# Second block of a two-block layer: the rows of decays and strengths of heads 1 to 3 come from memory instead of from products of TensorE

## What is computed

```
g = cumsum(g)                                     # log of the decay, within a chunk
decay  = exp(where(tril, g[:, None] - g[None, :], -inf))
lower  = where(strict, (k * beta) @ k.T * decay, 0)
a_mat  = lower + eye
u, w   = solve(a_mat, [v * beta, k * beta * exp(g)])
qk     = where(tril, q @ k.T * decay, 0)
# scan over the chunks
v_new  = u - w @ state
o      = (q * exp(g)) @ state + qk @ v_new
state  = state * exp(g_last) + (k * exp(g_last - g)).T @ v_new
```

## Time and profile before

| | us |
|---|---|
| median of 3 runs | 1174.02 (1173.92 to 1175.89) |
| the profiled execution | 1173.81 |
| its span | 1172.3 |
| TensorE busy | 1104.3 (94% of the span) |
| VectorE busy | 649.0 (55%) |
| ScalarE busy | 442.8 (38%) |
| GpSimd busy | 87.1 (7%) |
| mean granted TensorE clock | 0.972 of full speed |

### The profile page before, as it was taken

One profiled execution on the slowest core, in us unless ns is written; L12 is line 12 of the kernel. 1 busy time (PEld: TensorE's weight loads), 2 busy tenths in 40 slices (PEclk: granted clock), 3 DMA queues, 4 the chain that ended last, 5 costly groups with the idle time before them and its releaser, 6 DMA issues.

```text
span 1172.3 us, 15592 instructions
## 1 busy us (share of the span) xinstructions
PE 1104.3 (94%) x6320; PEld 876.1 (75%) x6320; DVE 649.0 (55%) x1099; ACT 442.8 (38%) x762; POOL 87.1 (7%) x76
## 2 busy tenths in 40 slices
PE   6999999999998999999999999688989999999898
PEld 4777877778786888888888887557767677677676
DVE  5444444445627688877772212753557467467474
ACT  5232323235444344444443222433244354254531
POOL 1000000000020000000001000000111121120210
PEclk9999999999998999999999999788999999899999
DMA  8112221212331233332322333121111111111101
GB/s 339 62 55 75 63 78 54 90 55 72 97 101 54 76 107 107 108 107 90 100 98 77 104 108 108 36 90 47 45 55 37 56 54 37 56 41 36 52 18 72
DMA packets 25254, 91.32 MB, mean 78 GB/s; under 512 B 2848, under 2 KB 3104, under 8 KB 25056
## 3 DMA queue, kind: packets, MB, share of 16 engines
q1 hardware_dynamic: 23040, 83.90, 22.5%
q0 software_dynamic: 704, 4.13, 0.9%
q10 hardware_dynamic: 1440, 2.31, 0.5%
HBM read 88.23 MB, written 2.10 MB: 77 GB/s over the span
## 4 chain that ended last, share of the span: by engine, by line
PE 82%; DVE 9%; ACT 5%; issue 3%; DMA 0%; POOL 0%; ACTq 0%; DVEq 0%
PE PS L497 20%; PE PS L500 19%; PE PS L498 19%; PE PS L590 2%; ACT Wh L1616 2%; PE PS L612 1%; PE PS L958 1%; PE PS L724 1%; PE PS L960 1%; PE PS L959 1%; DVE Wl L987 1%; PE PS L525 1%; PE PS L527 1%; PE PS L526 1%; PE PS L905 1%
## 5 line engine op out<-in xcount | busy, mean ns | idle before, releaser
L497 PE MATMUL PS<-Hh,Wh 128*128 128x512 f32 x856 | 356.1, 416 | 2.1 <-DVE Hl L1169 2.1
L500 PE MATMUL PS<-Hh,Wl 128*128 128x512 f32 x856 | 337.4, 394 | 0.0
L498 PE MATMUL PS<-Hl,Wh 128*128 128x512 f32 x856 | 337.2, 394 | 0.0
L987 DVE TENSOR_TENSOR Wl<-raw,Wh 128x1024 fp32r<-128x1024 f32 x156 | 190.0, 1223 | 209.6 <-ACT Wh L1616 208.2
L497 PEld LDWEIGHTS PS<-Hh,Wh 128*128 128x128 f32 x856 | 162.6, 190 | 50.2 <-issue 16.1
L500 PEld LDWEIGHTS PS<-Hh,Wl 128*128 128x128 f32 x856 | 162.5, 190 | 35.6
L1616 ACT ACTIVATE Wh<-raw 128x1024 fp32r<-128x1024 f32 x156 | 162.4, 1050 | 67.5 <-PE PS L500 48.1
L498 PEld LDWEIGHTS PS<-Hl,Wh 128*128 128x128 f32 x856 | 163.1, 191 | 28.4 <-issue 0.7
L497 PE MATMUL PS<-Ah,Wh 128*128 128x512 f32 x176 | 69.8, 396 | 0.0
L498 PE MATMUL PS<-Al,Wh 128*128 128x512 f32 x176 | 69.8, 396 | 0.0
L500 PE MATMUL PS<-Ah,Wl 128*128 128x512 f32 x176 | 69.8, 396 | 0.0
(11 more groups left out here) (308 smaller groups left out, 1581.7 us busy)
## 6 DMA issues: line engine op xcount, KB each, us to landing
raw<-in_w_units SPq DMA_DIRECT2D x156, 512.0 KB, 3.5
X<-in_x SPq DMA_DIRECT2D x4, 512.0 KB, 6.8
relb<-in_rel POOLq DMA_DIRECT2D x1, 2048.0 KB, 10.2
out<-X ACTq DMA_DIRECT2D x8, 256.0 KB, 2.0
window<-in_window POOLq DMA_DIRECT2D x1, 544.0 KB, 13.0
rope<-in_rope POOLq DMA_DIRECT2D x1, 512.0 KB, 4.4
mats<-in_mats POOLq DMA_DIRECT2D x1, 448.0 KB, 3.7
wgrp<-in_wgrp POOLq DMA_DIRECT2D x1, 256.0 KB, 10.9
```

The source lines that it names most:

```text
L497: pe.matmul(bank, Wh[:, s, w], rhs[0](r), start=first and j == 0, stop=False)
L498: pe.matmul(bank, Wh[:, s, w], rhs[1](r), start=False, stop=False)
L500: ins = pe.matmul(bank, Wl[:, s, w], rhs[0](r), start=False, stop=last and end)
L987: dv.tensor_tensor(Wl[:, s, :], raw[:, s, :], Wh[:, s, :].bitcast(F32), sub).then_inc(unit_split, 1)
```

## The change

For head 0 the two row products stay, with the sources now `glog` and `beta` themselves instead of a copy in `gs`. Behind them TensorE turns the columns `gcum` and `beta` of all heads at once (they now lie in one tensor, `gate_cols`), ScalarE copies the result to SBUF, and one transfer writes it to `gate_scratch` in memory. For heads 1 to 3 a transfer from there writes the row of cumulated g to all partitions of `DT` (issued at level 2 of the head before) and another the row of strengths to `Bm` (issued behind the head's last copy, `u`). VectorE then subtracts, masks and adds in place, in one group of three, at an earlier `yield` than before; ScalarE makes `EG` at the head of the stage. The `yield`s of `prep` are counted anew: for heads 1 to 3 all that follows stands one round earlier on every engine.

```diff
@@ TensorE, prep
-            pe.wait_ge(*prep_dv.at(i, "gs"))
-            row_of(b6, gs[:, 0, :], mat(K_UPPER)).then_inc(*prep_pe.tick(i, "g"))
-            row_of(b7, gs[:, 1, :], ident[:]).then_inc(*prep_pe.tick(i, "b"))
-            yield
-            yield
-            yield from idle(2)
-            yield
-            yield
+            if i == 0:
+                pe.wait_ge(*gate_dv.at(0, "beta_eg"))
+                row_of(b6, glog[:, 0, :], mat(K_UPPER)).then_inc(*gate_pe.tick(0, "g"))
+                row_of(b7, beta[:, 0, :], ident[:]).then_inc(*gate_pe.tick(0, "b"))
+                pe.transpose(PS[0:2 * N16, 5, 0:P], gate_cols[:].rearrange("p a h t -> p (a h t)"),
+                             ident[:]).then_inc(*gate_pe.tick(0, "back"))
+            yield from idle(6 if i == 0 else 5)
             pe.wait_ge(*prep_ac.at(i, "sq"))
...
@@ VectorE, prep
-            dv.tensor_copy(gs[:, 0, :], glog[:, i, :])
-            dv.tensor_copy(gs[:, 1, :], beta[:, i, :]).then_inc(*prep_dv.tick(i, "gs"))
-            yield
-            yield
-            dv.wait_ge(*prep_pe.at(i, "g"))
-            dv.tensor_tensor(tiles(DT[:]), tiles(b6), over_cols(gcum[:, i, :]),
+                dv.wait_ge(*prep_ac.at(i, "eg"))
+            else:
+                yield
+                dv.wait_ge(*gate_pe.at(0, "g"))
+            dv.tensor_tensor(tiles(DT[:]), tiles(DT[:] if i else b6), over_cols(gcum[:, i, :]),
                              sub).then_inc(*prep_dv.tick(i, "d"))
-            dv.wait_ge(*prep_pe.at(i, "b"))
-            dv.tensor_tensor(tiles(Bm[:]), tiles(b7), over_tiles(mat(K_STRICT_T)),
+            if i:
+                dv.wait_ge(strengths_loaded, 16 * i)
+            else:
+                dv.wait_ge(*gate_pe.at(0, "b"))
+            dv.tensor_tensor(tiles(Bm[:]), tiles(Bm[:] if i else b7), over_tiles(mat(K_STRICT_T)),
                              mult).then_inc(*prep_dv.tick(i, "bm"))
             dv.wait_ge(*prep_dv.at(i, "d"))
             dv.tensor_tensor(tiles(DT[:]), tiles(DT[:]), over_tiles(mat(K_NEG_T)),
                              add).then_inc(*prep_dv.tick(i, "dt"))
-            yield
-            yield from idle(2)
-            yield
-            yield
-            yield
+            yield from idle(6)
...
@@ ScalarE
+        def store_gates():
+            back = tmp[0:2 * N16, 1, 0:P]
+            ac.wait_ge(*gate_pe.at(0, "back"))
+            ac.activation(back, PS[0:2 * N16, 5, 0:P], ACT.Copy).then_inc(*gate_ac.tick(0, "back"))
+            ac.wait_ge(*gate_ac.at(0, "back"))
+            ac.dma_start(gate_scratch.rearrange("a h (t n) -> (a h t) n", t=NT),
+                         back).then_inc(gates_stored, 16)
+
+        def load_decays(i):
+            ac.dma_start(DT[:], gate_scratch[0, i, :].unsqueeze(0).to_broadcast(
+                [P, S])).then_inc(decays_loaded, 16)
+
+        def load_strengths(i):
+            ac.dma_start(Bm[:], gate_scratch[1, i, :].unsqueeze(0).to_broadcast(
+                [P, S])).then_inc(strengths_loaded, 16)
         def prep(st, i):
             if i:
                 silu_gates(i - 1)
-            yield
-            yield
-            ac.wait_ge(*prep_dv.at(i, "d"))
-            if i:
                 ac.wait_ge(*prep_gp.at(i - 1, "qg"))
-            ac.activation(EG[:], b6, ACT.Exp).then_inc(*prep_ac.tick(i, "eg"))
-            yield
+                ac.wait_ge(decays_loaded, 16 * i)
+                ac.activation(EG[:], DT[:], ACT.Exp).then_inc(*prep_ac.tick(i, "eg"))
+            yield
+            yield
+            if i == 0:
+                ac.wait_ge(*prep_dv.at(0, "d"))
+                ac.activation(EG[:], b6, ACT.Exp).then_inc(*prep_ac.tick(0, "eg"))
+                yield
             ac.wait_ge(*prep_dv.at(i, "dt"))
             ac.activation(DT[:], DT[:], ACT.Exp).then_inc(*prep_ac.tick(i, "dt"))
+            if i == 0:
+                store_gates()
...
+                if lv == 2 and i + 1 < GH:
+                    ac.wait_ge(*prep_dv.at(i, "at"))
+                    if i == 0:
+                        ac.wait_ge(gates_stored, 16)
+                    load_decays(i + 1)
...
             ac.activation(UU[:], b6, ACT.Copy).then_inc(*prep_ac.tick(i, "u"))
+            if i + 1 < GH:
+                load_strengths(i + 1)
```

30 lines of the change are left out of this document (16 added, 14 removed).

## The result

| | before | after |
|---|---|---|
| median of 6 runs on one chip, us | 1173.97 (1170.01 to 1175.89) | 1184.97 (1181.14 to 1188.85) |
| ratio, with 95% interval | | 1.0095 (1.0064 to 1.0126) |
| the profiled execution, us | 1173.81 | 1181.14 |
| its span, us | 1172.3 | 1179.4 |
| mean granted TensorE clock in it | 0.972 | 0.970 |

The changed kernel is 0.95% slower, some 11 us. The profiled execution is the fastest of its six. The forecast was 1174.9 us with 1169.2 to 1181.0 as its range, so it was wrong, and on the side of the rivals that end slower.

The account below looks back on a forecast made before the run. TensorE, with 82% of the chain that ended last, and its waits bound the kernel. Terms 0.8 - 1.76 - 1.3 + 1.6 + 2 x 0.8 + 2 x 0.3 - 0.5 = +1.0 us gave 1174.9 us, 80% range 1169.2 to 1181.0.

Parts of the forecast that it names:

- the rivals that end slower: Low clock behind head_Od waits, 1179.9 us (chance 0.22); loads of strengths landing late, 1180.9 us (chance 0.03).
- stage 0: TensorE's added turn 0.2, ScalarE's store issue 0.34 and copy 0.25, none hidden ahead of the squares: +0.8 us.
- start of stage 1: head_VN is ready 7 us ahead of use, so delays are hidden and the removed products gain in full: -1.76 us.
- start of stage 2: VectorE and GpSimd's chain may lengthen by 1 us, so the gain lies between 0.8 and 1.76: -1.3 us.
- start of stage 3: EG ahead of the rounding delays split, head_VN and scores; the start ends 1.6 us later despite fewer products.
- late in stages 1 and 2: VectorE takes level 5 ahead of Yc; TensorE's wait for head_Od grows to about 3 us: +0.8 us each stage.
- issues of ScalarE: Issuing a load at level 2 delays a ScalarE copy TensorE takes soon after: +0.3 us each for heads 1 and 2.
- behind the scores of stage 3: One more dense step under the 1.02 us wait before the scan gives 0.7 back, 0.2 lost inside: -0.5 us.
- Slower, by the clock: Rival: stage 1 also falls to the low clock behind head_Od, 5 us more, 1179.9 us; chance 0.22.
- the products' 5.3 us: Two row products of 0.88 us for each of three heads removed from TensorE: 5.3 us, 1.76 a stage.
- transfers are hidden: Loads of decays and strengths are issued early enough to land in time; without cover each would cost 2 to 4 us.

Follow-up runs that it names:

- f2: Changed kernel with the turn of the keys and the product of keys and queries one round later for heads 1 to 3; 1180.65 us.
- h1: Changed kernel with unused identity products in all nine TensorE waits of about 2 us or more after 780 us; 1170.58 us.
- e3: Kernel before, all its products kept and no transfers, with the preparation of heads 1 to 3 one round earlier; 1183.15 us.
- f1: Changed kernel with nine unused identity products in the waits for head_Od of heads 0 and 1 and for the last pair sums; 1177.72 us.
- g2: e2 with unused identity products in all nine TensorE waits of 2 us or more after 780 us; 1164.13 us.
- g3: Kernel before, with nothing of the change, and unused identity products in the same nine waits as g2; 1163.12 us.
- h3: e3 with unused identity products in all nine TensorE waits; 1173.86 us.
- e4: Changed kernel with nine unused identity products ahead of each head_Od (all four heads) and in the wait for the last pair sums; 1180.71 us.
- e1: Changed kernel with the preparation of heads 1 to 3 back in its old round, loads and removal of products kept; 1181.04 us.
- e2: e1 with ScalarE's EG of heads 1 to 3 also back behind the rounding of the weight unit; 1172.04 us.

## Why the prediction was wrong

Its terms, beside what the waits of the two profiled executions give (each new or longer wait, less the products of 1.76 us a stage):

| term | forecast | measured |
|---|---|---|
| stage 0 | +0.8 | +0.7 (1.99 to 2.66) |
| start of stage 1 | -1.76 | -1.8, no wait |
| start of stage 2 | -1.3 | -0.2 (new waits of 1.38 and 0.21) |
| start of stage 3 | +1.6 | +0.5 (1.05, 0.30, 0.96); +1.6 in f2 and h1, where the clock stayed up there |
| late in stages 1 and 2 | +1.6 | +1.2 (head_Od 2 x 0.8, two small waits of 0.2 gone) |
| issues of ScalarE | +0.6 | 0 |
| behind the scores of stage 3 | -0.5 | -1.1, in other waits than the one I named |
| product of keys and queries, level 1 | not in the sum | +4.2 (2 x 2.10) |
| sum | +1.0 | +3.5 (rest over all runs: +4.0) |
| clock | 0 | +6.6 over all runs |

**The step that failed first** is "Late in stages 1 and 2". It saw that everything from the sums on comes a round earlier and followed this at level 5 alone, because there the kernel before already waited. At level 1 the kernel before had no wait, so no row pointed there; but the shift is the same, and VectorE's split with its wait for the rounding stands ahead of the taking there too. e3 shows the wait with the products kept; f2, with two dense steps more ahead of the product, shortens it from 2.10 to 0.72 us. The term that had been put at nothing measured +4.2 us.

**The second** is the clock. The sum was made at the clock of the kernel before, and the rival "Slower, by the clock" put 5 us on one more stretch behind head_Od, with a chance of 0.22. The direction was right and its size near (6.6), but the place only in part: stage 1 did get a stretch behind head_Od, of 3.4 us and not 10, while the long one came behind the pair sums of stage 3. Its condition was also too narrow. f1, g2, g3 and h3 show that waits of 2.0 to 3.0 us can bring such stretches, so two added waits of 2.10 and two grown to 3.00 should have been charged with it. Which of the waits does so changes from kernel to kernel (L729's in e4 and h3, not in the changed kernel) and, it seems, from run to run: e1's runs spread from 1173.7 to 1185.1 us, with clocks from 0.975 to 0.965. The Trainium skill (TensorE: Matmul & The Clock Gate, section HAM oscillation) says that idle gaps between bursts of matmuls let the clock fall back; the trace agrees where the filled wait for head_Od keeps 1.00, but not every wait of that length has a stretch behind it.

**The third**, hidden in the total, is the start of stage 2. The prediction took TensorE's need there from the 15.70 us of the earlier trace rows, but 3.4 us of these ran at the lower level (the window from 945.6 to 961.3 has 0.89), which is 1.7 us of time. By this estimate TensorE needs 14.0 us at the upper level, without the products 12.2, and the chain of VectorE and GpSimd that the prediction put at 13.9 us (measured: 14.1, 947.39 to 961.53) ends last: nearly nothing of the 1.76 us is left, as the measured -0.2 says. It shows as a wait of 1.38 us for head_VN, which the prediction had followed in stage 3 alone.

**What was right**: that the products' 5.3 us would not arrive, the two terms of stage 0 and of head_Od, and the size of stage 3's start. That the starts of stages 2 and 3 come out right together (+0.3 forecast, +0.3 measured) is luck: with the clock up in both (h1) they are -0.2 and +1.6. In stage 3 part of the delay was hidden by the low clock itself: L889 took 2.08 us at 1038.86, and so TensorE came later to a wait that was 1.05 in place of 2.06 us. Not followed was that the late split would meet GpSimd's product in place of the tap; it took 1.85 us (at 1041.53), where 1.23 had been put. That transfers are hidden was right; that their issues cost 0.3 us was not.

Left open is how the loss divides between the early place and ScalarE's EG ahead of the rounding, and why the latter costs e1 as much as 5.4 us of clock part over e2. Its waits in stages 2 and 3 are longer by 3.5 us, and a link as in h3 is likely, but was not tried for itself.

## What to carry to other kernels

When a step is taken out of a staged program, list every hand-over that its round carried, those without a wait today above all, and look at each for what now stands ahead of it in the other engine's queue. Charge each added wait of TensorE of some 2 us twice, with its own length and with a chance of a stretch at the lower clock; split each run into span x (1 - clock) and the rest before explaining a difference. And where TensorE must wait, idle products in the wait can be worth more than the work that one can remove: here some 11 us for the former, 2 to 3 for the latter.
